# Residual stream with tokens on partitions, and the last down and out contractions swept half by half over all five token tiles

## The chip, the cores and the metric

The kernel runs on one core of one Trainium2 chip. The time is device microseconds of one execution, from the first to the last instruction of the core. The kernel before took 2431.77 us, the median of 3 runs (2429.27 to 2432.41).

## The reference

One inference step of a diffusion trunk of two layers (DEPTH = 2) with a width of 1024 (D_MODEL), over 128 prompt tokens and 512 latent tokens. Shift, scale and gate of every norm come from the conditioning vector, one for the prompt and one for the latent tokens. The attention and retention mixers between `h` and `branches` are left out here; the change does not touch them.

```python
def rmsnorm(x, gain):
    y = xf * lax.rsqrt(jnp.mean(xf * xf, axis=-1, keepdims=True) + NORM_EPS)
    return y * gain
...
    h = rmsnorm(x, g_mix) * (1 + scale1) + shift1      # then x_in = h @ w_in, four mixers
    ...
    gates = jax.nn.sigmoid((h @ p['w_gate'] + p['b_gate']).reshape(b, l, N_BRANCH, D_MODEL))
    mixed = jnp.sum(gates * branches, axis=2) @ p['w_out']
    x = x + gate1 * mixed
    h2 = rmsnorm(x, p['g_ffn']) * (1 + scale2) + shift2
    u = h2 @ p['w_up'] + p['b_up']                     # then a width-3 convolution over tokens
    a, gg = jnp.split(conv, 2, axis=-1)
    x = x + gate2 * ((jax.nn.silu(gg) * a) @ p['w_down'])
...
    y_prompt = rmsnorm(xp, g_final); y_sample = rmsnorm(xs, g_final)
```

## The kernel before, in words

There are 640 tokens in T = 5 tiles of 128: tile 0 is the prompt, tiles 1 to 4 the latent tokens. A width of 1024 is KD = 8 blocks of 128 channels. Every large product is made from three fp32r matmuls: the activation and the weight are each split into a high part (a rounded copy, `h_hi`, `a_hi`, `w_hi`) and a low part (the remainder, `h_lo`, `a_lo`, `w_lo`), and high by high, low by high and high by low are summed in PSUM. A weight unit is loaded into one of three `raw` buffers by the SP queue (1 MB), rounded into `w_hi` by ACT (line 1436) and subtracted into `w_lo` by POOL (line 767, four instructions); only the first two units of a layer's in-product are subtracted by DVE (line 1899). The order of every engine is written out by hand, with semaphores between the engines; SP loads the units in one fixed order (`weight_units`).

The residual `x` stands with channels on partitions, `[128, 8, 640]`. The norm over channels is therefore a sum over partitions: DVE squares and adds up the eight blocks (`add_square`, lines 2222 and 2224), PE sums over partitions with a vector of ones (`token_sums`, `part_sums`), ACT takes the root, DVE the reciprocal on a diagonal (line 1874), and PE spreads it over the partitions (`spread_rstd`, `spread_part`). DVE then makes scale times x times that (line 1883), ACT adds the shift and rounds into `h_hi` (line 1471), DVE makes `h_lo` (line 1891), block by block, and the first product (`in_product(0)`, line 914, groups of 512 columns per token tile) follows block by block. Layer 1's vectors (biases, gains, taps) are turned on PE at the boundary (`turn_vectors`, line 780), and the modulation of the norm (`mod_pair`, line 841, and `fold_pair`, line 850) is made around the start of each layer's first product.

Products on the residual's side have the weights as the stationary operand and the tokens as the moving one. The out product makes block m as two matmuls of 320 tokens for each of eight k; its last three blocks are split by tokens into 256 and 384, so that the first up tiles (`first_up`) can start on tokens 0 to 255 while the rest is added. The up and down products of the MLP run in three groups of up tiles, 8, 8 and 6 (`UP_GROUPS`), the down product of a group (`down_part`, columns of 322 and 320) two up tiles behind (`AHEAD`). DVE adds gate times the product to x (`add_to_x`, line 2230). At the start x is loaded with tokens on partitions and turned (40 transposes, line 791), and at the end it is turned back (40 transposes, line 1404) for the final norm (line 2333) and the stores.

## Time and profile before

| | us |
|---|---|
| median of 3 runs | 2431.77 |
| lowest, highest | 2429.27, 2432.41 |
| the profiled execution | 2432.2 |
| its span in the profile | 2430.4 |
| PE busy | 2363.8 |
| DVE, ACT, POOL busy | 1244.4, 879.1, 731.8 |
| mean granted clock of TensorE | 0.993 |

The profile page gives busy times and a chain of waits: the work that ended last, followed back to what released it at each step. The waits view tells how long PE stood idle and which engine's instruction released it. The timeline and the windows show one stretch. All times in them are from the start of the span, which is 1.8 us shorter than the execution's own time.

### The profile page before, as it was taken

To read this page: it belongs to the slowest core of one execution; us is meant where nothing else is said; L and a number is where in the kernel's file an instruction comes from. 1 tells how busy PE (TensorE), PEld (TensorE's weight loads), DVE (VectorE), ACT (ScalarE), POOL (GpSimd) and SP (SyncE) were. 2 spreads that over 40 slices of the span, in tenths; PEclk is the share of its full clock that TensorE was granted. 3 is DMA by queue.
4 is the path that set the end of the run, shared out by engine and by line. 5 is a ranking of instruction groups with operands and counts; after the bars stand their busy time and mean duration, and the time that the engine had idled before them with its cause. 6 is when DMAs were issued, how large, how long until landed. Compare 5 with 4: busy or idle time off the path is not lost.

```text
span 2430.4 us, 38405 instructions
## 1 busy us (share of the span) xinstructions
PE 2363.8 (97%) x16085; PEld 2144.0 (88%) x16085; DVE 1244.4 (51%) x2251; ACT 879.1 (36%) x1642; POOL 731.8 (30%) x500
## 2 busy tenths in 40 slices
PE   7999999999999999999999999999999999999998
PEld 5887787788999999999978878887889999999997
DVE  5426247534347762753763362673433677447356
ACT  4335245534324431332243352555343243223231
POOL 0321221101342453444312203210113435435432
PEclk9999999999999999999999999999999999999999
DMA  8413221222331322222271132312232312222211
GB/s 291 143 55 122 66 91 59 74 70 87 109 92 53 104 70 70 87 70 61 79 269 55 53 124 72 102 46 71 87 104 85 98 53 70 87 70 70 87 53 53
DMA packets 234154, 216.48 MB, mean 89 GB/s; under 512 B 8310, under 2 KB 217598, under 8 KB 233726
## 3 DMA queue, kind: packets, MB, share of 16 engines
q1 hardware_dynamic: 225911, 193.77, 25.0%
q10 hardware_dynamic: 8071, 20.25, 2.4%
q8 instruction: 128, 2.10, 0.3%
q14 instruction: 44, 0.36, 0.0%
HBM read 204.92 MB, written 9.08 MB: 88 GB/s over the span
## 4 chain that ended last, share of the span: by engine, by line
PE 88%; DVE 5%; ACT 3%; POOL 2%; issue 1%; DMA 0%; ACTq 0%; DVEq 0%
PE ps L819 58%; PE ps L914 11%; PE ps L968 4%; PE ps L1021 2%; POOL w_lo L767 2%; PE ps L1038 2%; PE ps L1000 2%; PE ps L1010 2%; PE ps L829 1%; ACT w_hi L1436 1%; DVE h_lo L1891 1%; PE ps L989 1%; DVE t L1883 1%; PE ps L859 1%; PE ps L1214 1%
## 5 line engine op out<-in xcount | busy, mean ns | idle before, releaser
L767 POOL TENSOR_TENSOR w_lo<-raw,w_hi 128x512 fp32r<-128x512 f32 x488 | 718.9, 1503 | 1664.3 <-ACT w_hi L1436 1048.8
L819 PE MATMUL ps<-h_hi,w_hi 128*128 128x320 f32 (+2 forms) x2368 | 618.4, 314 | 4.0 <-POOL w_lo L767 4.0
L819 PE MATMUL ps<-h_lo,w_hi 128*128 128x320 f32 (+2 forms) x2368 | 608.8, 310 | 0.0
L819 PE MATMUL ps<-h_hi,w_lo 128*128 128x320 f32 (+2 forms) x2368 | 608.7, 310 | 0.0
L819 PEld LDWEIGHTS ps<-h_hi,w_hi 128*128 128x128 f32 x2368 | 415.1, 189 | 8.8 <-issue 4.3
L819 PEld LDWEIGHTS ps<-h_lo,w_hi 128*128 128x128 f32 x2368 | 415.0, 189 | 0.8
L819 PEld LDWEIGHTS ps<-h_hi,w_lo 128*128 128x128 f32 x2368 | 415.0, 188 | 0.0
L1436 ACT ACTIVATE w_hi<-raw 128x2048 fp32r<-128x2048 f32 (+2 forms) x110 | 203.7, 1851 | 307.3 <-PE ps L819 219.0
L1986 DVE TENSOR_REDUCE stat<-ps 128x1 f32<-128x640 f32 (+3 forms) x160 | 107.9, 674 | 174.7 <-PE ps L1010 113.9
L914 PE MATMUL ps<-w_hi,h_hi 128*128 128x512 f32 (+1 forms) x480 | 182.8, 381 | 6.8 <-DVE h_lo L1891 3.8
L914 PE MATMUL ps<-w_hi,h_lo 128*128 128x512 f32 (+1 forms) x480 | 180.1, 375 | 0.0
L914 PE MATMUL ps<-w_lo,h_hi 128*128 128x512 f32 (+1 forms) x480 | 180.1, 375 | 0.0
L2230 DVE SCALAR_TENSOR_TENSOR x<-ps,mod,x 128x128 f32<-128x128 f32 (+4 forms) x192 | 72.9, 434 | 192.7 <-PE ps L819 192.0
L819 PE MATMUL ps<-a_hi,w_hi 128*128 128x322 f32 x704 | 162.6, 312 | 2.2 <-DVE a_lo L2297 1.4
L2282 DVE TENSOR_SCALAR conv<-u_pad,vcol 128x642 f32<-128x642 f32 x88 | 91.9, 1044 | 141.4 <-ACT u_pad L1788 139.8
L819 PE MATMUL ps<-a_hi,w_lo 128*128 128x322 f32 x704 | 161.7, 311 | 0.0
L819 PE MATMUL ps<-a_lo,w_hi 128*128 128x322 f32 x704 | 161.4, 310 | 0.0
L1796 ACT ACTIVATE usig<-conv 128x642 f32<-128x642 f32 x44 | 32.7, 744 | 261.3 <-DVE conv L2286 261.3
L968 PE MATMUL ps<-o_t,w_br 128*128 128x320 f32 x384 | 125.3, 450 | 0.0
L819 PEld LDWEIGHTS ps<-a_hi,w_hi 128*128 128x128 f32 x704 | 118.9, 190 | 3.3 <-DVE a_lo L2297 1.9
L2284 DVE SCALAR_TENSOR_TENSOR conv<-u_pad,vcol,conv 128x642 f32<-128x642 f32 x88 | 118.4, 1345 | 3.1
L819 PEld LDWEIGHTS ps<-a_lo,w_hi 128*128 128x128 f32 x704 | 118.8, 189 | 0.0
(299 smaller groups left out, 3330.0 us busy)
## 6 DMA issues: line engine op xcount, KB each, us to landing
raw<-in_w_mod SPq DMA_DIRECT2D x48, 1024.0 KB, 5.1
raw<-in_w_up SPq DMA_DIRECT2D x88, 512.0 KB, 4.6
raw<-in_w_gate SPq DMA_DIRECT2D x32, 1024.0 KB, 5.7
raw<-in_w_in SPq DMA_DIRECT2D x20, 1024.0 KB, 5.5
raw<-in_w_down SPq DMA_DIRECT2D x16, 1024.0 KB, 5.2
w_br<-in_w_branch ACTq DMA_DIRECT2D x8, 1024.0 KB, 5.0
raw<-in_w_out SPq DMA_DIRECT2D x8, 1024.0 KB, 5.2
raw<-in_w_down SPq DMA_DIRECT2D x8, 768.0 KB, 4.8
```

The costliest lines, as they stand in the source:

```text
L767: ins = nc.gpsimd.tensor_tensor(w_lo[part_slot(li, s)][:, c0:c1], raw[u % RAW][:, c0:c1], w_hi[part_slot(li, s)][:, c0:c1].bitcast(F32), A ...
L819: ins = mm(out, w_at(w_hl[wi]), at_(x_hl[xi]), start=first and q == 0, stop=final and q == 2)
L914: last = mm(bank(b, 0, n), (h_hi, h_lo)[xi][:, k, t * P:(t + 1) * P], w_hl[wi][:, k4, :], start=k == 0 and q == 0, stop=k == KD - 1 and q ...
L968: last = mm(bank(FILL_BANK[("branch", q)], 0, HALF), w_br[:, k, m * P:(m + 1) * P], o_t[n % 2][:, k, half * HALF:(half + 1) * HALF], start ...
L1000: last = mm(bank(2 * m2, col, col + n), query(br, t, h, m2), keys(br, h, m2, k0, n), start=True, stop=True)
L1010: last = mm(bank(2 * (m % 2), col, col + n), query(br, t, h, 0), keys(br, h, 0, k0, n), start=True, stop=True)
L1021: last = mm(ps[64 * odd:64 * odd + 64, 6 * BANK + 64 * h:6 * BANK + 64 * h + P], values(br, b, h + odd), turned(a_ + odd)[:, j, :], start= ...
L1436: act_(w_hi[part_slot(li, s)][:, 0:n], raw[u % RAW][:, 0:n], ACT.Copy).then_inc(hi_done.sem, 1)
L1986: V.tensor_reduce(stat[:, 0, col], bank(b, 0, nk), AX.X, ALU.max).then_inc(vstep.sem, 1)
L2230: ins = stt(x[:, k, c0:c0 + n], src, mod[:, gate0 + k, w:w + 1], x[:, k, c0:c0 + n], ALU.mult, ALU.add)
L2282: ts(cv, u[:, 0:PADDED], col(WCONV[0]), col(BCONV), ALU.mult, ALU.add).then_inc(vstep.sem, 1)
L2284: stt(cv, u[:, 1:1 + PADDED], col(WCONV[1]), cv, ALU.mult, ALU.add).then_inc(vstep.sem, 1)
```

## The change

The residual becomes `[128, 5, 1024]`, tokens on partitions; `acc`, the mixers' sum, gets a name of its own in the same memory. In the out and down products the activations (128 tokens of `mix_hi` or `a_hi`) are now stationary and 512 columns of the weights moving, so a weight unit is a half of the output columns (`dh`) by a half of the contraction (`kh`). The last output half of both, `dh = 1`, is made in two sweeps, each over all five tiles (`SWEEPS`). The norm is made per tile of tokens: ACT squares with a running sum and takes the root, DVE the reciprocal, ACT scales, PE turns eight blocks into PSUM (`turn_rows`), DVE modulates from PSUM, ACT rounds, DVE subtracts. Sums, diagonals and spreads go, as do the transposes at the start and at the end. The gates along channels are written to DRAM as rows and loaded back broadcast over partitions (`gate_rows`, `grow`). The four mod pairs of layer 1 are made among the down products of layer 0 (`PAIR_AT`), with their loads at the same place of SP's order. `ACT_SLOTS` goes from 12 to 10. The core of the diff:

```diff
-ACT_SLOTS = 12
+ACT_SLOTS = 10
...
+PAIR_AT = {(0, 0, 0): 0, (0, 0, 1): 1, (1, 0, 0): 2, (1, 0, 1): 3}
...
+ROW_BANK = ((0, 1, 2, 3, 4), (0, 1, 5, 6, 7))
+TURN_BANK = {"in": ((2, 3), (1, 4), (3, 5), (6, 7), (4, 5)), "ffn": ((2, 3), (0, 1), (4, 5), (2, 3), (6, 7))}
+SWEEPS = ((0, (0, 1, 2, 3, 4)), (1, (0, 1, 2, 3, 4)))
...
+                def turn_rows(layer, which, t):
+                    pe.wait_ge(xn_done.sem, ROW_BASE[layer, which] + t + 1)
+                    if t >= 2:
+                        pe.wait_ge(t1_done.sem, TURN_BASE[layer, which] + t - 1)
+                    if which == "in" and t == 3:
+                        pe.wait_ge(x_down.sem, counts(layer - 1)(x_down, n_down))
+                    if which == "ffn" and t == 4:
+                        pe.wait_ge(x_out.sem, counts(layer)(x_out, 2 * T))
+                    for k in range(KD):
+                        last = tr(bank(TURN_BANK[which][t][k // 4], k % 4 * P, k % 4 * P + P), xn[:, t % 2, k * P:(k + 1) * P], ident)
+                    last.then_inc(turn_mm.sem, 1)
...
+                if li == 0:
+                    turn_channels(0)
+                    mod_pair(0, 0)
+                    turn_channels(1)
...
+                else:
+                    first_product({(0, 0): lambda: turn_rows(li, "in", 3), (0, 1): lambda: turn_rows(li, "in", 4)})
+                    turn_vectors(7)
+                    pe.wait_ge(vec_done.sem, now(vec_done, 1))
                 in_product(1)
...
+                def out_sweep(dh, kh, tiles):
...
+                            for q, (xi, wi) in enumerate(((0, 0), (0, 1), (1, 0))):
+                                last = mm(bank(b), (mix_hi, mix_lo)[xi][:, k, row_cols(t)], w_hl[wi][:, k4, :],
+                                          start=k == 0 and q == 0, stop=k == KD - 1 and q == 2)
...
+                        if dh == 1 and (kh, t) in ((1, 2), (1, 3), (1, 4)):
+                            turn_rows(li, "ffn", {(1, 2): 0, (1, 3): 1, (1, 4): 2}[kh, t])
...
+                out_sweep(0, 0, range(T))
+                out_sweep(0, 1, range(T))
+                for kh, tiles in SWEEPS:
+                    out_sweep(1, kh, tiles)
...
+                        if (j, tokens, k) == (0, 0, 3):
+                            turn_rows(li, "ffn", 3)
+                        if (j, tokens, k) == (1, 0, 0):
+                            turn_rows(li, "ffn", 4)
...
+                        at_ = slice(t * P + (t > 0), t * P + (t > 0) + P)
+                        for k4 in range(nk):
+                            k = kh * nk + k4
+                            if dh == 0 and t == 0:
+                                pe.wait_ge(al_done.sem, now(al_done, j0 + k + 1))
+                            sl = (j0 + k) % ACT_SLOTS
+                            for q, (xi, wi) in enumerate(((0, 0), (0, 1), (1, 0))):
+                                last = mm(bank(b), (a_hi, a_lo)[xi][:, sl, at_], w_hl[wi][:, k4, :],
+                                          start=k == 0 and q == 0, stop=k == nj - 1 and q == 2)
...
+                    down_sweep(g, dh, kh, range(T))
+                    if (g, dh, kh) in PAIR_AT and li + 1 < DEPTH:
+                        pe.wait_ge(up_done.sem, now(up_done, min(FFT, sum(UP_GROUPS[g]) + AHEAD)))
+                        if (g, dh, kh) == (0, 0, 0):
+                            turn_mod_vectors()
+                        mod_pair(li + 1, PAIR_AT[g, dh, kh])
...
+                def norm_rows(layer, which, add, between):
+
+                    rstd = lambda t: row_rstd(ROW_BASE[layer, which] + t + 1, t)
+                    add(0)
+                    add(1)
+                    rstd(0)
+                    rstd(1)
+                    add(2)
+                    rstd(2)
+                    row_modulated(layer, which, 0)
+                    row_modulated(layer, which, 1)
+                    between()
+                    row_low(layer, which, 0)
+                    row_low(layer, which, 1)
+                    add(3)
+                    row_modulated(layer, which, 2)
+                    rstd(3)
+                    row_low(layer, which, 2)
+                    add(4)
+                    rstd(4)
...
+                def add_rows(t, dh, parts, gated, done, n):
+
+                    cols = slice(dh * BANK, dh * BANK + BANK)
+                    tt(parts[:, n % 2, :], bank(ROW_BANK[dh][t]), grow[:, min(t, 1), cols], ALU.mult).then_inc(gated.sem, 1)
+                    ve.wait_ge(gated.sem, now(gated, n))
+                    tt(x[:, t, cols], x[:, t, cols], parts[:, n % 2, :], ALU.add).then_inc(done.sem, 1)
```

PE at the boundary of the two layers, before: the last down matmul, the vectors' transposes (line 780), a mod pair (841), the sums (866), the fold (850), the spread (873), another pair and the first in-product (914).

```order
L819 MATMUL ps<-a_hi,w_lo_57 128x320
L780 MATMUL ps<-const,rows 128x96 [waits rows_loaded,x_after_mlp]
...
L841 MATMUL ps<-raw_52,cond_c 32x256 [waits raw_loaded0]
...
L866 MATMUL ps<-ones,ss 128x1 [waits squares_ready0,x_after_mlp]
...
L850 MATMUL ps<-const,mod_row 128x4 [waits mod_row_ready]
...
L873 MATMUL ps<-diag,ones 128x128 [waits rstd_diagonal,mod_ready]
...
L914 MATMUL ps<-w_hi_56,h_hi 128x512 [waits w_low_by_vector,h_ready,x_ready,vectors_ready]
```

PE at the same place, now: the turns of rows (line 889) stand behind the last down tiles (line 1386) and behind the first in tiles (905), the vectors' transposes (801) behind the whole first product, and the second in-product (938) behind them.

```order
L1386 MATMUL ps<-w_hi_56,a_lo 128x512
L889 MATMUL ps<-const,xn 128x128 [waits row_normed]
...
L889 MATMUL ps<-const,xn 128x128 [waits modulated,row_normed]
...
L905 MATMUL ps<-w_hi_57,h_hi 128x512 [waits h_ready,w_low_by_vector,w_low_ready]
...
L889 MATMUL ps<-const,xn 128x128 [waits x_after_mlp,modulated,row_normed]
...
L801 MATMUL ps<-const,rows 128x96
...
L938 MATMUL ps<-w_hi_57,h_hi 128x512 [waits w_low_ready,vectors_ready]
```

The mod pairs, sums and spread are gone from there; the vectors have moved from ahead of the first product to behind it.

DVE at the same boundary, now: residual adds (lines 2293 and 2295), reciprocals (1885), modulation from PSUM (1941), the weights' low half (1980), `h_lo` (1947).

```order
L1941 TENSOR_SCALAR hn<-ps,scl,mod 128x128 [waits normed_turned]
L1941 TENSOR_SCALAR hn<-ps,scl,mod 128x128 x7
L1980 TENSOR_TENSOR w_lo_59<-raw_54,w_hi_57 128x1024 [waits w_high_ready]
L1947 TENSOR_TENSOR h_lo<-hn,h_hi 128x8x128 [waits h_high] x2
L2293 TENSOR_TENSOR part_down<-ps,grow 128x512 [waits down_product]
L2295 TENSOR_TENSOR x<-x,part_down 128x512 [waits down_gated]
...
L1873 COPY vcol<-ps 128x317 [waits vectors_transposed,vector_step]
...
L2110 COPY decay<-decay 64x4 [waits small_loaded,vector_step]
```

The adds of tiles 3 and 4 stand behind the low parts of tiles 0 and 1; before, all adds stood ahead of the first modulation.

ACT in the norm of the MLP, now: the weight round (line 1455) stands between the scaled rows (1497) and the first rounded copies (1502).

```order
L1490 ACTIVATE xn,st_82<-x 128x1024 [waits x_after_mixers]
L1492 ACT_TABLE_LOAD
L1492 ACTIVATE st_82<-st_82,eps_c 128x1 [waits row_squares]
...
L1497 ACTIVATE xn<-x,st_82 128x1024 [waits row_rstd] x2
...
L1455 ACTIVATE w_hi_56<-raw_55 128x2048 [waits out_first_half,raw_loaded2]
L1502 ACTIVATE h_hi<-hn 128x8x128 [waits modulated] x2
```

Before, ACT read and rounded block by block (line 1471) behind one root for all tiles.

## Rows read from the trace of the kernel before

**Rows 1.** The page, its span, part 1 and part 4 (shares of the chain).

```profile
span 2430.4 us, 38405 instructions
...
PE 2363.8 (97%) x16085; PEld 2144.0 (88%) x16085; DVE 1244.4 (51%) x2251; ACT 879.1 (36%) x1642; POOL 731.8 (30%) x500
...
PE 88%; DVE 5%; ACT 3%; POOL 2%; issue 1%; DMA 0%; ACTq 0%; DVEq 0%
```

**Rows 2.** Waits of PE, whole span: total us, times, longest us.

```profile
PE ps L819 <- POOL w_lo L767: 4.9, 6, 1.3
...
PE ps L914 <- DVE h_lo L1891: 3.8, 2, 3.6
```

**Rows 3.** Chain of waits, pieces: start us, us, what, times in row.

```profile
679.90 5.14 PE ps L819 x35
...
790.85 381.98 PE ps L819 x2592
...
1186.89 2.05 PE ps L819 x12
...
1195.59 21.67 PE ps L819 x144
...
1227.86 1.62 PE ps L914 x6
...
1253.13 0.08 DVE decay L2041
...
1256.22 5.03 POOL w_lo L767 x4
1261.30 27.49 PE ps L914 x120
```

**Rows 4.** Chain of waits at the start, columns as in Rows 3.

```profile
13.59 6.39 PE ps L791 x40
...
28.30 6.16 PE ps L914 x15
34.45 1.86 PE ps L841 x32
...
61.23 5.04 POOL w_lo L767 x4
```

**Rows 5.** Timelines, DVE at 740 and PE at 775: start us, us, engine, line.

```profile
740.08 2.04 DVE L1891 SCALAR_TENSOR_TENSOR h_lo<-t,mod,h_hi 128x128 fp32r<-128x128 f32 x2
742.15 0.60 DVE L1883 SCALAR_TENSOR_TENSOR t<-x,scl,ps 128x128 f32<-128x128 f32 x2
742.67 0.61 DVE L1891 SCALAR_TENSOR_TENSOR h_lo<-t,mod,h_hi 128x128 fp32r<-128x128 f32 x2
...
775.87 0.45 PE L819 MATMUL ps<-h_hi,w_hi 128*128 128x320 f32 x2
```

**Rows 6.** Groups by form: ACT in 12:29, then DVE whole: busy us, mean ns.

```profile
L1417 ACT ACTIVATE y_tm<-x_tm 128x1024 f32<-128x1024 f32 x5 | 5.2, 1046 | 5.9 <-DMA x_tm<-in_x_sample 5.9
...
L1482 ACT ACT_TABLE_LOAD x1 | 1.3, 1283 | 0.0
...
L2224 DVE TENSOR_TENSOR ss<-ss,sq 128x640 f32<-128x640 f32 x22 | 28.4, 1291 | 0.8
...
L2138 DVE TENSOR_TENSOR st_dec<-ps,dmask 128x512 f32<-128x512 f32 x10 | 6.9, 692 | 30.6 <-PE ps L1101 30.6
```

**Rows 7.** Windows: us, busy PE, PEld, DVE, ACT, POOL, granted clock, DMA, GB/s.

```profile
28.00:34.00 6.00, 5.70 (x14) 4.53 (x15) 2.74 (x4) 0.00 (x0) 0.00 (x0) 0.53 0.53 177
...
1217.00:1262.00 45.00, 41.52 (x293) 31.17 (x292) 31.78 (x79) 19.38 (x33) 5.02 (x4) 1.00 0.87 314
```

**Rows 8.** Page, part 3: packets, MB, share of 16 engines.

```profile
q1 hardware_dynamic: 225911, 193.77, 25.0%
```

**Rows 9.** Timeline of the tail, columns as in Rows 5.

```profile
2411.78 0.31 PE L819 MATMUL ps<-a_hi,w_lo 128*128 128x320 f32 x1
...
2422.02 5.08 DVE L2333 SCALAR_TENSOR_TENSOR y_tm<-ps,st,g_fin 128x1024 f32<-128x1024 f32 x4 [0.35 <-PE ps L1404]
```

815 lines of the change are left out of this document (388 added, 427 removed).

## The prediction

> **What bounds the kernel now.** I read the page first, then PE's waits, then the chain of waits at the places that the change touches. PE is busy 97% of the span and the chain is PE for 88% [rows 1]; its largest waits on other engines' work inside the layers come to 4.9 and 3.8 us in total [rows 2]. So the time is PE's work in order plus the few places where PE has no work that is ready, and the change is to be judged by both. The profiled execution took 2432.2 us (span 2430.4); the sum is made against it, and the median 2431.8 lies 0.4 below. I count from marks: start of the second in-product (66.3 = 61.23 + 5.04, when POOL's w_lo is ready) [rows 4]; start of the out product (685.0 = 679.90 + 5.14) and start of the third up tile (775.9) [rows 3, 5]; start of layer 1's second in-product (1261.3) [rows 3]; last down matmul (2412.1) and end (2430.4) [rows 9, 1].
>
> **PE's rates.** A 512-column matmul takes 27.49/120 = 0.229 us; an up or down matmul of 320 or 322 columns 381.98/2592 = 0.147 in the long piece and 21.67/144 = 0.150 in the last downs, where all are downs [rows 3]; a transpose 6.39/40 = 0.16 [rows 4].
>
> **Down and up.** Before, a layer has 1056 down matmuls: at 0.149, between the two rates, 157.3 us. After, 660 of 512 columns: 151.1, so -6.2 a layer. The third group starts with the last up tile's activation missing: that tile ends at 1172.8 and its product starts at 1186.9 [rows 3], 14.0 us, of which PE fills all but 0.7 with other down work. After, one tile's wait for a_lo is in the first sweep: only its five other k steps and nothing of m 0 to 2 lie ahead; I take the cover that is left as 11.7 (five 0.23 us triples, and two up tiles' tail) and so a wait of 2.3: +1.6. One POOL wait of 0.4 there goes. The mod pairs of layer 1 move into layer 0's downs: 4 x 2.0 = +8.0 (an old pair is 1.86 [rows 4]; a new one has twice the matmuls at a quarter of the columns; bounds 0.9 to 3.7). Their loads stand ahead of two down weight loads in SP's queue: a load lands some 5 us after its issue; between 0 and 5 I take 1.4 each, as the slot comes free one tile earlier: +2.8. Together 2 x (-6.2 + 1.6 - 0.4) + 8.0 + 2.8 = **+0.8**.
>
> **Out to first ups.** Before 775.9 - 685.0 = 90.8. After: 192 matmuls of 512 columns until tile 0 of the last sweep is done, 44.0. From there I wrote a timetable of the orders shown above. Prices: residual multiply and add 0.7 each (512 from PSUM 0.69; the 640 in SBUF has a mean of 1.29, mixed of 0.83 alone and about 1.8 beside POOL) [rows 6]; Square with its read 1.2 and the table load 1.28 once, which stands on the path behind the first Square [rows 6]; Sqrt 0.27, reciprocal 0.17, scaling 1.05, the copy to h_hi 1.05, h_lo 1.24; eight transposes 1.28; the eight modulations of a tile 2.1. For these eight the trace has no tensor_scalar from PSUM: the scalar_tensor_tensor from PSUM is 0.30 for each 128 columns [rows 5], so 2.4 at most, and 1.6 at 0.2 each as the low end; I take 0.26. The Trainium skill (VectorE: DVE Perf Modes, Why PSUM operands drop a tier) says that an fp32 operand in PSUM keeps DVE at 1x, where one in SBUF could go at 2x; by it the high end would hold, 1.2 us more in each of three stages. No run here shows it yet.
> The timetable, from the end of tile 0: x is summed at 1.7, its square at 2.9, root at 4.5 (table load between), xn at 7.1. PE is through with tiles 1 and 2 at 5.5, so it waits 1.7 for the first turn. Tile 4 is done at 15.3, turn 2 at 16.6. DVE modulates tiles 0 and 1 until 14.9, then h_hi of both (ACT, 16.0, behind the weight round) and h_lo until 19.5, with POOL in its way; so first_up waits 3.0. DVE is behind from then on: tile 3 of x is added only at 20.9, tile 4 at 28.1. PE waits 2.0 before turn 3, 1.8 before turn 4, and 1.6 for h_lo of tile 4 (38.9). End of the four first ups: 55.9, of it 10.1 of waits. 44.0 + 55.9 - 90.8 = +9.1; the POOL wait before the fourth up tile (0.7 of 4.9 [rows 2]) goes, as PE comes to that tile later than its weights. (The wait of 1.0 for gprod at the start of the out product goes too; it is in the 90.8.) **+8.4 a layer, +16.8.**
>
> **Layer boundary.** Before, from the end of the last down matmul (1195.59 + 21.67 = 1217.3) to 1261.3: 44.0 [rows 3]. After, the same timetable with tiles of nine matmuls (2.06 us, so less cover): a wait of 3.1 before the first turn, 3.0 before the first in tile (its weights' low half is DVE's too), and 8.0 before turn 3, which needs the banks of down tiles 3 and 4 and therefore DVE's last residual add, done only at 28.8. The first product ends at 56.2; with the tiles after tile 0 taken off (4 x 2.06 = 8.2), 48.0 behind the last down matmul. Then the vectors: PE turns all 317 columns now, DVE copies them, and only behind that DVE starts the decay chain that ACT waits for before it rounds the next weights; 1253.13 to 1261.30 is 8.2 us [rows 3], which before lay beside PE's work and is now beside nothing. With 1.6 for turning and copying: 9.8. 48.0 + 9.8 - 44.0 = +13.8. The clock: at the start PE waits 3.6 us for h_lo [rows 2] and then runs at a granted 0.53 [rows 7], so at 1.2 GHz for a time: 15 matmuls took 6.16 instead of 3.44 [rows 4], 2.7 us. In the boundary before, with PE busy 41.5 of 45 us, it stayed at 1.00 [rows 7]. I count one such fall, behind the 9 us wait, +2.7. **+16.5.** By the Trainium skill (TensorE: Matmul & The Clock Gate, HAM oscillation) every longer idle gap between bursts brings the clock back to its low level; the 8.0 wait would then cost as much again, and the first start [rows 7] agrees with it.
>
> **Start.** The sums by token fall away, but channels are turned in the middle of the product. The last scaled row is there at about 23.3 (squares end 19.7, five roots, table load), the first turn, the pair, modulation, high and low give a first matmul at 30.5 against 28.30 [rows 4]. The product itself: 120 x 0.229 with its slow beginning 30.4, three pairs 6.0, six turns of five 4.8 (bank 5 alone, each waits for the one before), 2.2 of wait for channel 6; end 73.9. The vector and weight chain of 8.2 starts with the last h_lo and ends at 75.8, against 66.3: **+9.5.**
>
> **Tail.** Before 2430.4 - 2412.1 = 18.3, with sums, table load, 40 transposes and four products of 1.27 [rows 9]. After, no PE work: DVE has 1.4 + 0.2 + 1.28 for each of five tiles, begins at the end of tile 0 (-8.2) and ends 7.9 behind the last matmul; the last store needs the 3.3 that it needs now. 11.2: **-7.1.**
>
> **Sum.** 0.8 + 16.8 + 16.5 + 9.5 - 7.1 = +36.5: 2468.7, at the median 2468.
>
> **Rivals.** (a) *The row work hides* (faster): if ACT and DVE finish each row before PE needs it, the waits of 10.1 twice, 14.1 + 9.8 + 2.7, 4.1 at the start and 2.8 go, 53.7 in all; 2415. It decides at h_lo of tiles 0 and 1 before 16.6, when PE is through with its turns; mine is at 19.5, and the other tiles stand behind it in DVE's order. Half of the waits gone would be 2441.
> (b) *The clock falls at more waits*: also at 8.0, at 3.1 and 3.0, and in both ffn norms: 2 to 6 times 2.7 more, 2474 to 2484.
> (c) *Cheaper rows*: modulation 1.6, POOL not in DVE's way (4 less in three stages), the mod pair at 0.9 to 1.5, no queue wait: 2446 to 2460. Against the middle part stands [rows 5]: a low pair is 2.04 beside POOL's work and 0.61 without.
> (d) *The gate rows block SP's queue*: 4,096 elements of 4 bytes per layer ahead of the w_out loads. 0.25 x 16 engines x 2430 us over 225,911 packets [rows 8] is 43 ns each, 11 us over 16 engines; the load has some 23 us of slack in my reading of its issue. If they went over a few engines only, 44 us or more: w_out late by 20 in each layer, 2508.
> (e) *Nothing moves*: the wider matmuls and the tail pay for what is left of the waits. That needs two thirds of the 53.7 to be gone: 2432.
>
> **Chances.** Forecast (2460 to 2473) 0.45; (b) 0.18; (c) 0.20; (d) 0.05; (a) 0.09; (e) 0.03. The range leaves out (a) and (e) and most of (d): 2442 to 2486. A measurement of this kernel can tell about 0.2% (4.9 us) from no change: faster 0.09, same 0.03, slower 0.88.
>
> **What would show it.** Right: PE waits for h_lo, xn and x (down add) at every norm, some 10 us in each ffn norm and some 24 at the boundary; the granted clock below 1.00 at the boundary; DVE's eight modulations near 2.1; a tail of 11; out plus down matmuls at 0.229. Wrong: turn 3 waits for nothing (DVE's order was cheaper), or no wait before the second in-product, or 512-column downs slower than 0.229, which read their weights from odd columns of a_hi.

## The result, and the profile after

The changed kernel takes 2496.81 us, the median of 4 runs (2493.3 to 2501.8), against 2430.52 for the kernel before beside it (4 runs): the ratio is 1.0274, with an interval of 1.0254 to 1.0294. The change costs 66 us. The profiled execution has a span of 2495.4 us, 65.0 above the 2430.4 of [rows 1].

The page's span, part 1 and part 4, as in [rows 1]:

```profile
span 2495.4 us, 37639 instructions
...
PE 2360.1 (95%) x15742; PEld 2066.5 (83%) x15742; DVE 1234.7 (49%) x2169; ACT 901.8 (36%) x1644; POOL 735.3 (29%) x506
...
PE 85%; DVE 6%; ACT 4%; DMA 3%; POOL 1%; issue 1%; SPq 0%; DVEq 0%; ACTq 0%
```

PE is busy for 3.7 us less than before and the span is 65 us longer: all of the loss is time in which PE is idle, 68.7 us more of it. The waits that the view lists add up to 124.2 us, against 60.7; the other 5 us are gaps that it does not list. The waits view of PE, whole span (total us, times, longest us), its largest rows:

```profile
PE ps L831 <- DVE w_lo L2276: 17.2, 2, 10.4
PE ps L831 <- DVE h_lo L1947: 12.1, 4, 3.5
PE ps L938 <- POOL w_lo L788: 11.0, 2, 9.1
PE ps L876 <- DVE xn L1891: 9.7, 1, 9.7
...
PE ps L889 <- DVE x L2295: 6.4, 1, 6.4
...
PE ps L1386 <- POOL w_lo L788: 4.8, 2, 2.7
PE ps L1386 <- DVE a_lo L2334: 4.4, 2, 2.2
```

The row for h_lo at the first up tiles is 12.1 us now; the same view of the kernel before has for it (its line 819):

```profile
PE ps L819 <- DVE h_lo L1891: 1.7, 4, 0.7
```

The h_lo row of 3.8 in [rows 2] is another one, that of the in-products. The rows for h_lo, xn and x are the norm by rows, L938 on POOL is the wait for the vectors, the two rows of line 1386 are the downs: the forecast named all of these waits. It had nothing for the first row: 17.2 us in two waits for the low half of the last branch's weights (line 2276).

The second thing that it had too small is PE's clock. Over windows of 10 us I summed PE's busy time times one less the granted clock, the share of the time that was given up at a lower clock: 24.9 us, against 13.5 before. So PE's work at full clock would have got about 15 us shorter (-3.7 in busy time, and 11.4 of lower clock hidden in it), and its listed waits got 63.5 us longer.

The chain of waits, pieces at the marks of [rows 3, 4] (start us, us, what):

```profile
77.64 27.51 PE ps L938 x120
...
646.04 58.62 PE ps L831 x384
704.66 44.81 PE ps L1314 x192
...
788.74 129.68 PE ps L831 x864
...
1316.41 29.00 PE ps L938 x120
...
1946.51 44.81 PE ps L1314 x192
```

The second in-product of layer 0 starts at 77.6 (before 66.3), the out product at 704.7 (685.0), the second part of the first ups (line 831, x864) at 788.7, layer 1's second in-product at 1316.4 (1261.3), its out product at 1946.5 (1879.9). From these and the starts of the third up tiles (805.6 and 2047.5, before 775.9 and 1970.7) the loss by stretch:

| stretch | before | after | difference | forecast |
|---|---|---|---|---|
| start to second in-product | 66.3 | 77.6 | +11.3 | +9.5 |
| to out product, layer 0 | 618.7 | 627.0 | +8.3 | 0 |
| to third up tile | 90.8 | 101.0 | +10.1 | +9.1 |
| to last down matmul (turns and waits inside the last sweep taken off) | 441.4 | 452.3 | +10.9 | +5.1 |
| to layer 1's second in-product | 44.0 | 58.5 | +14.5 | +16.5 |
| to out product, layer 1 | 618.6 | 630.1 | +11.5 | 0 |
| to third up tile | 90.8 | 101.0 | +10.1 | +9.1 |
| to last down matmul (the same) | 441.4 | 437.3 | -4.1 | -5.7 |
| to the end | 18.3 | 10.6 | -7.7 | -7.1 |
| all | 2430.4 | 2495.4 | +65.0 | +36.5 |

The two stretches that the forecast had at nothing make 19.8 of the 28.5 us that it missed. (By place, 2.7 of the 16.5 forecast for the boundary, the slow clock behind the vectors' wait, belong to the stretch after it: so the boundary had 13.8 and took 14.5, and the second of the two stretches had 2.7 and took 11.5.)

**The branch weights.** The timeline at 618 to 650 (start us, us, engine, line, operation):

```profile
618.72 6.02 SPq L757 DMA_DIRECT2D gate_rows<-mod  x4
...
621.65 0.40 ACTq L1571 DMA_DIRECT2D w_br<-in_w_branch  x1
...
641.66 1.91 ACT L1795 ACTIVATE w_hi<-w_br 128x2048 fp32r<-128x2048 f32 x1 [12.18 <-DMA w_br<-in_w_branch]
...
643.61 2.29 DVE L2276 TENSOR_TENSOR w_lo<-w_br,w_hi 128x2048 fp32r<-128x2048 f32 x1 [16.95 <-ACT w_hi L1795]
...
646.04 0.87 PE L831 MATMUL ps<-o_hi,w_hi 128*128 128x320 f32 x2 [10.35 <-DVE w_lo L2276]
```

SP issues the four writes of the gate rows at 618.7, ACT the load of the last branch's weights at 621.7. The load has landed at 641.7; ACT rounds it, DVE subtracts, and PE has waited 10.35 us at 646.0. The DMA view of 600:660 (KB each, median us to landing), and below it the same view of the kernel before at 590:650:

```profile
w_br<-in_w_branch ACTq DMA_DIRECT2D x1, 1024.0 KB, 20.0
...
gate_rows<-mod SPq DMA_DIRECT2D x4, 4.0 KB, 15.9
```
```profile
w_br<-in_w_branch ACTq DMA_DIRECT2D x1, 1024.0 KB, 4.8
```

The writes move 4 KB each and take 15.9 us; the load beside them takes 20.0 instead of 4.8. It came 15.2 later and PE waited 10.4, so this load had about 4.9 us of slack. In layer 1 the load took 16.5 us and PE waited 6.9. The 15.9 is the median of the four writes, each of 1,024 elements; the landings of all four (least, median, longest, from each one's issue):

```profile
DMA to landing us min/median/max: 12.1/15.9/21.4
```

The last of them, issued at 624.4, landed at 643.5, 24.8 us after the first was issued. The wait also costs clock: the 384 matmuls behind it took 58.62 us (59.11 in layer 1), where at the rate of the same product in e1 below (70.54 us for 480) they take 56.4.

**The norm by rows.** The chain at the layer boundary:

```profile
1252.57 1.28 ACT L1492
...
1259.48 5.09 DVE hn L1941 x16
...
1266.14 2.27 DVE h_lo L1947 x2
...
1276.38 1.81 DVE x L2295
...
1278.33 1.94 PE ps L889 x8
...
1311.33 4.95 POOL w_lo L788 x4
```

In order: ACT's table load behind the first Square, two tiles' modulations on DVE (5.09 us for 16), their h_lo, the last residual add (1.81 us while POOL makes a low half from 1276.37 on, 0.69 two tiles before with POOL idle), and only then PE's turn 3 at 1278.33. At the end POOL makes the low half of the second in-product's weights, done at 1316.3; PE, through with the vectors' turn, has waited 9.1 for it. Groups of DVE by form (busy us, mean ns):

```profile
L2295 DVE TENSOR_TENSOR x<-x,part_down 128x512 f32<-128x512 f32 x60 | 57.6, 959 | 2.0
...
L1941 DVE TENSOR_SCALAR hn<-ps,scl,mod 128x128 f32<-128x128 f32 x120 | 39.2, 400 | 0.4 <-PE ps L889 0.4
...
L1947 DVE TENSOR_TENSOR h_lo<-hn,h_hi 128x1024 fp32r<-128x1024 f32 x15 | 21.1, 1423 | 13.2 <-ACT h_hi L1502 13.2
```

The windows view (us, busy PE, PEld, DVE, ACT, POOL, granted clock, DMA share, GB/s) shows where the clock goes:

```profile
640.00:660.00 20.00, 13.96 (x81) 13.99 (x82) 7.54 (x7) 6.66 (x6) 4.97 (x4) 0.74 0.42 127
1260.00:1280.00 20.00, 9.81 (x45) 7.73 (x43) 16.11 (x33) 11.34 (x14) 6.14 (x5) 0.80 0.16 52
1316.00:1326.00 10.00, 9.59 (x36) 7.84 (x37) 7.40 (x11) 4.09 (x15) 5.22 (x5) 0.81 0.68 210
```

Each of these windows holds one of the waits above or follows it, and has a mean granted clock of 0.74 to 0.81, so part of it was run at 1.2 GHz; the boundary before stood at 1.00 [rows 7].

### The profile page after: what moved, and what is told of

The parts are those of the page before. It is cut to its first block, busy times and chain, and to the rows that moved or that the text cites. A ratio compares the mean times of both kernels' runs of the same rounds, so it can differ in the third digit from the quotient of the medians.

```text
span 2495.4 us, 37639 instructions
## 1 busy us (share of the span) xinstructions
PE 2360.1 (95%) x15742; PEld 2066.5 (83%) x15742; DVE 1234.7 (49%) x2169; ACT 901.8 (36%) x1644; POOL 735.3 (29%) x506
## 3 DMA queue, kind: packets, MB, share of 16 engines
q1 hardware_dynamic: 218871, 193.80, 24.9%
## 4 chain that ended last, share of the span: by engine, by line
PE 85%; DVE 6%; ACT 4%; DMA 3%; POOL 1%; issue 1%; SPq 0%; DVEq 0%; ACTq 0%
PE ps L831 42%; PE ps L938 10%; PE ps L1386 10%; PE ps L992 4%; PE ps L1314 4%; PE ps L1045 2%; PE ps L1062 2%; PE ps L1024 2%; PE ps L1034 2%; DMA w_br<-in_w_branch 1%; POOL w_lo L788 1%; DVE hn L1941 1%; PE ps L842 1%; PE ps L905 1%; DMA raw<-in_w_down 1%
## 5 line engine op out<-in xcount | busy, mean ns | idle before, releaser
L1386 PE MATMUL ps<-w_hi,a_hi 128*128 128x512 f32 x440 | 174.8, 397 | 9.2 <-POOL w_lo L788 4.8
L938 PE MATMUL ps<-w_hi,h_hi 128*128 128x512 f32 (+1 forms) x440 | 166.7, 379 | 17.4 <-POOL w_lo L788 11.0
L1386 PE MATMUL ps<-w_lo,a_hi 128*128 128x512 f32 x440 | 174.2, 396 | 0.0
L1386 PE MATMUL ps<-w_hi,a_lo 128*128 128x512 f32 x440 | 174.1, 396 | 0.0
L2319 DVE TENSOR_SCALAR conv<-u_pad,vcol 128x642 f32<-128x642 f32 x88 | 90.1, 1024 | 156.3 <-ACT u_pad L1830 154.7
L938 PE MATMUL ps<-w_lo,h_hi 128*128 128x512 f32 (+1 forms) x440 | 164.2, 373 | 0.0
L938 PE MATMUL ps<-w_hi,h_lo 128*128 128x512 f32 (+1 forms) x440 | 164.2, 373 | 0.0
L1830 ACT ACTIVATE u_pad<-ps,vcol 128x128 f32<-128x128 f32 (+3 forms) x264 | 91.6, 447 | 91.7 <-PE ps L831 91.7
L2323 DVE SCALAR_TENSOR_TENSOR conv<-u_pad,vcol,conv 128x642 f32<-128x642 f32 x88 | 116.7, 1326 | 3.1
L2321 DVE SCALAR_TENSOR_TENSOR conv<-u_pad,vcol,conv 128x642 f32<-128x642 f32 x88 | 116.6, 1325 | 3.1
L1600 ACT ACTIVATE probs<-ps,stat 128x640 f32<-128x640 f32 (+3 forms) x136 | 90.2, 664 | 67.7 <-DVE stat L2063 67.1
```

What stands on the lines that cost most here:

```text
L938: last = mm(bank(b, 0, n), (h_hi, h_lo)[xi][:, k, t * P:(t + 1) * P], w_hl[wi][:, k4, :], start=k == 0 and q == 0, stop=k == KD - 1 and q ...
L1386: last = mm(bank(b), (a_hi, a_lo)[xi][:, sl, at_], w_hl[wi][:, k4, :], start=k == 0 and q == 0, stop=k == nj - 1 and q == 2)
L1600: act_(prob(m)[:, 0:nk], bank(score_bank(m), 0, nk), ACT.Exp, bias=bias, scale=SCALES[br], accum_out=stat[:, 2, m % 8:m % 8 + 1]).then_inc ...
L1830: ins = act_(u[:, d0:d0 + n], bank(b, c0, c0 + n), ACT.Identity, bias=bias)
L2321: stt(cv, u[:, 1:1 + PADDED], col(WCONV[1]), cv, ALU.mult, ALU.add).then_inc(vstep.sem, 1)
L2323: ins = stt(cv, u[:, 2:2 + PADDED], col(WCONV[2]), cv, ALU.mult, ALU.add)
```

## The experiments

All times are medians of 4 runs beside runs of the kernel before on the same chip. e1 to e4 shared a chip, and so did e5 to e8, e9 to e12, and e13 with e14; between these groups compare the ratios. An interval reaches 0.0015 to 0.0024 to either side, 4 to 6 us, so many of the smaller steps are read from the stretches of the trace. The last two columns are of the profiled execution, in us: what PE gave up at a lower clock, as above, and the sum of PE's waits. That execution is not always near the median: e5's took 2475.1 us, the longest of its four, e8's 2464.3 and e14's 2455.1, the shortest of theirs.

| kernel | median us | ratio, 95% interval | at low clock | waits of PE |
|---|---|---|---|---|
| before | 2429.3 to 2430.5 | 1 | 13.5 | 60.7 |
| changed | 2496.8 | 1.0274, 1.0254 to 1.0294 | 24.9 | 124.2 |
| e1 rows behind w_br | 2482.5 | 1.0214, 1.0198 to 1.0229 | 20.9 | 109.2 |
| e2 rows twice | 2510.5 | 1.0330, 1.0311 to 1.0348 | 26.2 | 135.9 |
| e3 vectors early | 2492.7 | 1.0255, 1.0236 to 1.0273 | 28.7 | 115.3 |
| e4 sweeps split | 2498.2 | 1.0275, 1.0259 to 1.0290 | 28.9 | 124.5 |
| e5 = e1 + e3 | 2469.3 | 1.0164, 1.0147 to 1.0181 | 21.5 | 98.3 |
| e6 = e5 + turns later | 2474.7 | 1.0183, 1.0168 to 1.0198 | 25.7 | 97.0 |
| e7 = e6 + modulate first | 2471.8 | 1.0172, 1.0157 to 1.0188 | 21.1 | 98.3 |
| e8 = e5 + sweeps split | 2468.7 | 1.0160, 1.0143 to 1.0177 | 15.6 | 102.0 |
| e9 = e5 + idle filled | 2470.9 | 1.0172, 1.0155 to 1.0189 | 18.5 | 88.5 |
| e10 = e5 + table ahead | 2472.8 | 1.0172, 1.0157 to 1.0188 | 27.1 | 97.0 |
| e11 = e5 + second pair in sweep | 2468.6 | 1.0158, 1.0142 to 1.0173 | 23.1 | 97.5 |
| e12 = e8 + e10, e11, shorter e9 | 2461.8 | 1.0136, 1.0113 to 1.0160 | 14.1 | 90.2 |
| e13 = e5 + first pair in sweep | 2466.1 | 1.0149, 1.0134 to 1.0165 | 24.2 | 95.2 |
| e14 = e8 + e10, e13, e7's order on DVE | 2461.4 | 1.0133, 1.0116 to 1.0150 | 14.7 | 94.3 |

### The gate rows behind the branch weights (e1, e2)

```diff
                         sp.wait_ge(mod_done.sem, now(mod_done, 20))
+                        sp.wait_ge(branch_loaded.sem, now(branch_loaded, 16 * NB))
                         for v in range(2):
```

> One edit to the changed kernel: SP waits until the last branch weights (w_br) have landed before it issues the four writes of the gate rows. Theory A (the 4-byte writes share the rings with the w_br load and made it land after 20.0 us instead of 4.8): PE's waits of 10.4 and 6.9 us for DVE's w_lo go, the load lands in about 5 us, and the time falls by 15 to 18 us to about 2480. The first w_out load then comes later (writes 16 us, load 5) but has some 50 us until it is needed, so no new wait. Rival B (the w_br load is late because ACT issues it later in the changed kernel, or because of the weight loads beside it): the load still takes about 20 us and the time stays at 2497. Rival C (w_out becomes late instead): the waits go, but PE waits some 10 us before the out product, net change under 8 us.

Measured 2482.5, -14.3. The DMA view of e1 at 600:660:

```profile
w_br<-in_w_branch ACTq DMA_DIRECT2D x1, 1024.0 KB, 5.0
```

and the chain of waits, the same product as at 646.04 above:

```profile
626.00 70.54 PE ps L832 x480
```

The load lands in 5.0 us, and the wait of PE is gone in both layers. The stretches from the second in-product to the out product take 617.3 and 619.9 us, against 627.0 and 630.1 with the change and 618.7 and 618.6 before: the whole of the unforeseen loss in these stretches was due to the writes beside this load, and 19.9 us come back. Of them some 5 do not show in the median. In the profile the start is 1.6 us longer, the downs of layer 0 0.6 and the last downs 1.5; for the last the granted clock is lower (0.90 and 0.93 in 2430:2450, where the changed kernel has 1.00), for the start it is not, and that stays open. Theory A holds, with 14.3 us for the 15 to 18 expected. Rivals B and C fall: PE does not wait ahead of the out product. With no load beside them the elements of layer 0 are moved within 12 us: the DMA view of e1 at 631:643 counts 4,155 packets under 512 B. That is the price that the forecast had for them, 11 us.

e2 issues each write a second time, into a DRAM tensor that nothing reads:

```diff
+                                sp.dma_start(gate_again[li, v, c_].rearrange("(k p) -> p k", p=P), mod[:, 16 + 24 * v:24 + 24 * v, c_],
+                                             allow_slow_non_contiguous=True).then_inc(again.sem, 16)
```

> One edit to the changed kernel: each of the four gate-row writes per layer is issued twice, the second time to another DRAM tensor that nobody reads. Theory A (these writes hold the rings, about 16 us for 4,096 elements): 4,096 more elements hold them some 16 us longer, the w_br load lands after about 36 us, and PE waits some 16 us longer in each layer: 2496.8 + 2 x 16 = about 2529. Rival B (the cause of the late load is another one): within 4 us of 2497. If the load overtakes the second half of the writes, the rise is less than half of theory A's.

```profile
PE ps L835 <- DVE w_lo L2280: 27.1, 2, 15.4
```
```profile
w_br<-in_w_branch ACTq DMA_DIRECT2D x1, 1024.0 KB, 21.3
...
gate_rows<-mod SPq DMA_DIRECT2D x4, 4.0 KB, 28.1
```

and of layer 1, at 1840:1900 (16.5 with the change):

```profile
w_br<-in_w_branch ACTq DMA_DIRECT2D x1, 1024.0 KB, 25.1
```

The timeline in layer 0:

```profile
622.04 0.40 ACTq L1575 DMA_DIRECT2D w_br<-in_w_branch  x1
...
625.22 18.00 SPq L758 DMA_DIRECT2D gate_rows<-mod  x1
...
643.39 1.91 ACT L1799 ACTIVATE w_hi<-w_br 128x2048 fp32r<-128x2048 f32 x1 [13.51 <-DMA w_br<-in_w_branch]
```

The waits grow from 17.2 to 27.1 us and the time by 13.7. The direction is theory A's, the size is not: it is less than half of the 32, the case that the expectation names for a load that overtakes the second half of the writes. SP gets four of the eight transfers out by 625 and then stands in the issue of the next for 18.00 us, until 643.2, when the load has landed too (21.3 after its issue). My reading, which no run tests by itself: the load is held up only by the writes that were issued by then, four as in the changed kernel, and the rest falls on what comes later: the w_out loads take 21.3 us here. That fits layer 0, where the load takes 1.3 us more and PE's wait grows from 10.4 to 11.7. It does not explain layer 1: there SP stands in its fifth issue for 19.6 us just so, and yet the load takes 8.6 us more and the wait grows from 6.9 to 15.4. What sets the size stays open. Twice the elements cost 10 us more of PE's wait, not 32.

### Layer 1's vectors (e3, e5)

```diff
+                    def early_vectors():
+                        pe.wait_ge(t1_done.sem, TURN_BASE[li, "in"] + 4)
+                        turn_vectors(7)
-                    first_product({(0, 0): lambda: turn_rows(li, "in", 3), (0, 1): lambda: turn_rows(li, "in", 4)})
-                    turn_vectors(7)
+                    first_product({(0, 0): lambda: turn_rows(li, "in", 3), (0, 1): lambda: turn_rows(li, "in", 4), (0, 4): early_vectors})
```

> One edit to the changed kernel: PE turns layer 1's vectors behind the first half of the first product (after tile 4 of it, and when DVE has read row tile 3 from the same bank) instead of behind the whole product. Forecast's theory (DVE's copy and the decay chain, ACT's round and POOL's w_lo are 9.1 us that nothing covers, and the clock falls behind this wait): the wait of 9.1 before the second in-product goes, the slow clock behind it too (29.0 us for 120 matmuls back to 27.5), so -9 to -11 us, about 2486. Rival (another release sets that round: the raw load, the slot of the first in weights, or DVE's h_lo of tile 4, done late): the wait shrinks by less than 4 us, 2493 to 2497.

Measured 2492.7, only 4.1 less, and with runs from 2487.4 to 2498.2. In the trace the wait of 9.1 for POOL is gone, and 120 matmuls of the second in-product take 27.20 us instead of 29.00:

```profile
1165.52 56.33 PE ps L831 x384
...
1315.50 27.20 PE ps L938 x120
```

From 1165.52 (the last up tiles) to there it is 150.0 us, against 158.8 with the change: -8.8 in place, close to the -9 to -11 expected. From there to layer 1's out product it is 3.6 less, half of it the faster matmuls. What the median does not show was given back where the kernels do not differ: +4.7 between the first layer's second in-product and its out product, +2.8 in its ups and downs. Why, these two traces do not say for certain; the time given up at a lower clock is 3.8 higher in e3. e5 puts both edits together:

> The changed kernel with two edits together: gate rows written only when w_br has landed (-14.4 us alone) and layer 1's vectors turned behind the first half of the first product. Alone the second moved its own stretch (from the third group's up tiles to the second in-product) by 8.8 us in the trace, but the median by 4.1 only. Theory (the gains are of separate places and add; the missing part was scatter of the w_br wait and of the clock behind it, which the first edit takes out): 2482.5 - 9 = 2473.5, and runs that scatter by less than 4 us. Rival (the vectors' gain is given back elsewhere): 2478 to 2482.

2469.3: -27.5 from the changed kernel, -13.2 from e1, more than the two medians alone add up to (14.3 + 4.1) and near what the stretches add up to (19.9 + 8.8). In e5's own trace the boundary is 152.5 us, 6.3 less than with the change and not 8.8: the last downs ahead of the norm took 23.33 us for 93 matmuls there, 21.88 with the change. The theory's number (2473.5) lies 4 above; that the runs scatter by less than 4 us was wrong (2466.8 to 2475.1).

### The split of the sweeps (e4, e8)

```diff
-SWEEPS = ((0, (0, 1, 2, 3, 4)), (1, (0, 1, 2, 3, 4)))
+SWEEPS = ((0, (0, 1, 2)), (1, (0, 1, 2)), (0, (3, 4)), (1, (3, 4)))
```

> One edit to the changed kernel: the last output half of out and down, and the first in-product of layer 1, run over tiles 0 to 2 (both halves of the contraction) and then over tiles 3 and 4, instead of each half over all five. Theory (sweeping each half over all five tiles leaves only two tiles' work between the end of tile 0 and the first turn, and DVE gets tiles 0 to 2 too late): tile 0 is done 6 x 2.75 us of matmuls, not 4 x 2.75, before the end in out, so 5.5 us (out) and 4.1 us (down) more cover in each of the two ffn norms, the boundary and the tail; the waits for xn at turn 1 or later and for h_lo of tiles 0 and 1 go (3.5 + 3.8 and parts of the rest), together -3 to -5 us per norm, -10 to -14 in all: about 2485. Rival (DVE's total work per norm is the limit, not when tile 0 is done; or the weights' slots are released later and rounds come late): within 4 us of 2497, or slower by some 5 us for late w_lo of the first up tiles.

2498.2, no change. In place: from the start of the out product to the second part of the first ups 82.4 us in both layers, where it was 84.1; the boundary 157.6 for 158.8; the tail's stretch 1.4 less. So the split is worth 1.7, 1.2, 1.7 and 1.4, together 6, half of what the theory had. The waits for h_lo go from 12.1 to 9.4, and the one for DVE's last add grows from 6.4 to 7.9: with more work of PE ahead, DVE's own list of work is what is late. The rival is right on the median and in its reason. On top of e5:

> The kernel of the two edits together (gate rows behind w_br, vectors earlier), with the last out and down halves and the first product run over tiles 0 to 2 and then 3 and 4, as in e4. Alone this edit left the median where it was, though its stretches were 1.7, 1.2, 1.7 and 1.4 us shorter in the trace. Theory (the gain is real and was hidden by scatter of the w_br wait and the clock): -5 to -6 us against the kernel of the two edits, about 2468. Rival (no gain, as measured alone): within 2 us of that kernel.

2468.7 against 2469.3: not to be told from nothing by the median; the two stretches from the out product to the first ups are again 1.7 shorter each.

### The order inside the norm (e6, e7, e10)

e6 turns row tiles 3 and 4 behind tiles 1 and 2 of the first product (`(0, 1)` and `(0, 2)` in the dictionary); e7 also calls `row_modulated(layer, which, 0)` ahead of `rstd(2)` on DVE; e10 puts `act_(st5[:, 3, 0:1], eps_c[:], ACT.Sqrt)` ahead of `rms(0)` on ACT.

> The kernel of the two edits together (gate rows behind w_br, vectors earlier), with the turns of row tiles 3 and 4 in layer 1's first product one tile later (behind tiles 1 and 2 instead of 0 and 1). Theory (the wait of 6.4 us before turn 3 is DVE's last residual add; PE could do tile 1 in it): PE fills 2.75 us of that wait, and row tiles 3 and 4 are still in time, -2 to -3 us against that kernel. Rival (tiles 3 and 4 then come late by as much, since DVE's chain behind turn 3 sets their h_lo): within 1 us of it.

> The kernel before this one (gate rows behind w_br, vectors earlier, turns one tile later), with one more edit in all three norms by rows: DVE modulates row tile 0 before it takes the reciprocal of tile 2, for which it waits some 2 us while tile 0's turn is done. Theory (DVE's order, not its work, makes h_lo of tiles 0 and 1 late): -1 to -2 us in each of three norms, -3 to -6 in all, with PE's waits for h_lo lower by that. Rival (ACT's chain for tile 2 gets late by the modulation of 2.6 us and turn 2 waits instead): 0 to +3 us.

> The kernel of e5 with one root of a constant put ahead of the first Square in each norm by rows, so that ACT loads its table of 1.28 us while it waits for x. Theory (the table load stands on the path from the end of tile 0 to the first turn): PE's wait before the first turn falls by 1.3 us in each of three norms (2.6 to 1.3 in the boundary), and h_lo of tiles 0 and 1 by up to as much: -2.5 to -4 us in all. Rival (turn 0 earlier gives nothing as the later waits for h_lo and x grow by the same): within 1 us of e5 (2469).

e6: 2474.7, +5.4 on e5, and 154.1 us from the last up tiles to the second in-product where e5 has 152.5. The wait for x falls from 5.4 to 3.8 and the one for h_lo rises from 2.7 to 5.0: filling the wait helps nothing, as the tiles behind it are late by more. The theory's sign was wrong; the rival gives the reason, but had the time within 1 us. (The wait for x before turn 3 is 5.4 us in e5 and 6.3 to 6.6 in e1, e11 and e13, which have the same code there.) e7: 2471.8; its ffn stretch is 83.8 for 84.1, the boundary 153.7 for 154.1: 0.3 to 0.4 each, not 1 to 2. e10: 2472.8, slower by the median than e5 within the intervals; the boundary is 150.8 (-1.7), while the waits for h_lo in the ffn norms stay at 6.0. The table load is on the path to the first turn and hardly on the path to the first product. All three theories had too much. What they leave is that DVE's work in sequence (0.69 + 0.69, 2.55, 1.23 a tile) sets the end: the three show that these other orders gain little, and no run has less work on DVE, so this is argued and not shown.

### The clock (e9)

```diff
+                            if t == 4:
+                                for _ in range(12):
+                                    mm(bank(2), mix_hi[:, 0, 0:P], mix_hi[:, 1, 0:512], start=True, stop=True)
```

and the same with 10 and 20 matmuls in the boundary.

> The kernel of e5 (gate rows behind w_br, vectors earlier) with matmuls that nobody reads put on PE into three of its waits: 12 behind turn 2 of each ffn norm (2.7 us into the waits of 3.4 and 2.6 for h_lo), 10 at the same place of the boundary and 20 ahead of the wait of 5.4 us for turn 3. They are shorter than the waits, so they delay nothing that is on the path; what changes is that PE is not idle. Theory (part of the lost time is the granted clock, which falls behind these waits: 21.5 us of PE time given up at low clock in e5's trace against 13.5 in the kernel before): the granted clock in the boundary and behind the ffn norms stays nearer to 1.00 and the time falls by 3 to 6 us, 2463 to 2466. Rival (the clock does not depend on such short waits, or the falls come at other places): within 1.5 us of e5, or +1 to +3 where a filler overshoots its wait.

2470.9 against 2469.3. The time given up at the low clock goes from 21.5 to 18.5 us, and the boundary (152.7 for 152.5) and the ffn stretches (84.1 for 84.1) take what they took: PE's waits fall to 88.5, as the filling counts as work, and nothing comes of it. In the boundary the granted clock did rise, in windows of 10 us from 0.83, 0.67 and 0.81 (e5, from 1258) to 1.00, 0.83 and 1.00 (e9, from 1252), and the time did not fall: there the end is not set by PE's clock, and the theory falls. In the ffn norms the clock stayed where it was (0.83 in 761:771 of e5, 0.84 in 757:767 of e9), so that half was not tested. What the falls elsewhere cost, this run does not say.

### The mod pairs in layer 0's downs (e11, e13)

e11 makes the second pair of a group, e13 the first one, from within `down_sweep`, behind tile 3 and tile 2. The edit of e13, which stands ahead of the sweep's line for tile 3:

```diff
+                        if not kh and dh == 0 and t == 2 and (g, 0, 0) in PAIR_AT and li + 1 < DEPTH:
+                            pe.wait_ge(up_done.sem, now(up_done, min(FFT, sum(UP_GROUPS[g]) + AHEAD)))
+                            if g == 0:
+                                turn_mod_vectors()
+                            mod_pair(li + 1, PAIR_AT[g, 0, 0])
```

> The kernel of e5 with the second mod pair of each of the first two down groups of layer 0 put behind tile 3 of its sweep instead of behind tile 4, so that PE frees the raw buffer 2.75 us earlier in which the next down unit is loaded. Theory (the waits of 2.7 and 2.1 us for POOL's w_lo in layer 0's downs come from that buffer, held by the mod units until PE reads them): both waits go or shrink below 0.5, -4 us: about 2465. Rival (the load waits for SP's order or the mod loads' own arrival, not for PE's read): the waits stay and the time is within 1 us of e5.

The waits stay (4.2 for 5.0), 2468.6: the theory falls.

> The kernel of e5 with the first mod pair of each of the first two down groups of layer 0 (and the turn of its vectors) put behind tile 2 of the first sweep instead of behind tile 4. Theory (SP's queue waits for PE's read of the first pair's raw buffers before it issues the second pair's loads, and the third down unit's load stands behind those; the trace has that load 10.8 us from the first pair's read): the read comes 5.5 us earlier, so the two waits for POOL's w_lo (2.8 and 2.2 us) go below 0.5 each: -4 to -5 us, about 2465. Rival (as with the second pair, the waits stay at 4 to 5 us in all): within 1.5 us of e5, 2468 to 2471.

The chain of the changed kernel at 900:960, and below it that of e13:

```profile
918.42 13.88 PE ps L1386 x60
...
932.50 1.97 PE ps L855 x128
...
934.90 10.75 DMA raw<-in_w_down
...
945.67 1.93 ACT w_hi L1455
...
947.67 5.42 POOL w_lo L788 x4
...
953.13 6.92 PE ps L1386 x22
```
```profile
914.43 8.34 PE ps L1391 x36
...
922.97 1.92 PE ps L856 x128
924.89 19.74 PE ps L1391 x84
944.63 1.92 PE ps L856 x128
946.55 13.63 PE ps L1391 x58
```

With the change PE's read of the first pair (932.5) lets SP issue the second pair's loads and behind them the down weights, which land 10.75 us later; round and low half end at 953.1. In e13 the chain is PE from one end to the other, and both waits are gone. The ratio is 1.0149 where e5 has 1.0164, inside the intervals of the two; the trace settles it: from the second part of the first ups to the last up tiles of layer 0 it is 364.0 us for 370.6, of which 1.6 is one piece of matmuls that ran at a low clock in e5. The pairs themselves, 4 x 1.97 us, stay.

### All together (e12, e14)

> Gate rows behind w_br, vectors earlier, sweeps split 3 and 2, root table ahead (in the tail too), second pairs inside the sweep, and shorter fillers (4 behind turn 2 in each ffn norm, 3 in the boundary, 20 ahead of turn 3). Theory (the gains add): e8's 2468.7 less 3 (table), 4 (pairs), 3 (clock): about 2459, so still some 28 us slower than the kernel before, since the row norms' waits of about 8 us each, the start and the four moved pairs stay. Rival (more gains than that, each wait removed also keeps the clock up): 2450 or below; it would have to be below 2425 to beat the kernel before, which I do not expect.

> Gate rows behind w_br, vectors earlier, sweeps split 3 and 2, modulation of tile 0 ahead of tile 2's reciprocal, root table ahead (tail too), first pairs inside the sweep, no fillers. Theory (the parts add, and the fillers of e12 gave nothing): e8's 2468.7 less 3 (modulation), 2 (table), 4 (pairs): about 2460, like e12's 2461.8. Rival (without fillers the clock falls more often and takes it back): 2465 to 2469. Neither beats the kernel before.

2461.8 and 2461.4, 2.8 and 1.4 above what was expected (e12 holds the edits of e1, e3, e4, e9 with fewer matmuls, e10 with the same load ahead of the tail, and e11; e14 those of e1, e3, e4, e7's order on DVE, e10 and the tail, and e13). e14 comes out as fast as e12 without any filling. With e14 the changed kernel has 35 us of its 66 back and is 1.33% slower than the kernel before. The traces have less of it: the profiled execution of e14 is its fastest, with a span of 2453.3 us, 22.9 above the kernel before. In it PE waits 94.3 us instead of 60.7, 33.6 more, and is busy 13.2 us less. The largest of them that belong to the change are those of the rows' chain (10.3 for xn, 9.4 for h_lo, 6.3 for x), 9.3 for the first scaled rows and 5.3 ahead of the second in-products. No version ran that beats the kernel before.

## Why the prediction was wrong, point by point

The sign was right and the size was not: +36.5 forecast, +65 and +66 measured, 11 us beyond the range's end.

- **The gate rows' writes** are the step that failed. Rival (d) had them, asked only what they do to SP's own queue, and priced them at 43 ns an element, 11 us, with 23 us of slack in front of the w_out loads; the forecast itself put them at nothing. The price alone was fair (12 us in e1), and PE did not wait for w_out. But they hold up more than the queue of their issuer: ACT's load of the last branch's weights, issued 3 us behind the first of them, landed after 20.0 us (16.5 in layer 1) instead of 4.8, and the writes themselves took 24.8 from the first issue to the last landing. The chain of that load (round, subtract) had 4.9 us of slack. Asking which loads of other queues are in flight at that time, and which of those is needed next, was left out. Cost: 19.8 us in the stretches (e1). Without them the kernel takes 2482.5, inside the range. By what means the writes slow the load, no run shows.
- **Layer 0's downs**: +10.9, forecast +5.1. The waits for the down weights were 2.7 and 2.1 us, where 2.8 in all was forecast, by the mechanism named (SP's order), to which e13 adds that SP stands there until PE has read the first pair. A moved pair is 1.97, as taken. The 512-column matmul took 55.69/240 = 0.232 here, not 0.229: 2 us a layer. The rest, some 2 us, is at a low clock: 29.69 us for 120 matmuls at 953.13, where the next such piece has 28.11.
- **The last a_lo**: a wait of 2.2 us in each layer, forecast 2.3. Layer 1's downs, -4.1 for -5.7, differ by about the same: 0.232 makes 2.0. The prediction gave slower downs as a sign that reading weights from odd columns costs time; the out product, which does not read from there, has 44.81/192 = 0.233 too, so that is not the reason.
- **Out to first ups**: 56.1 us from the end of tile 0 to the third up tile, forecast 55.9; first turn after 6.8, forecast 7.2; waits for h_lo of 3.5 and 2.5 forecast as 3.0 and 1.6, 9.0 of waits in all for 10.1. The eight modulations are 2.55, for 2.1 taken, and above the high end of 2.4. There the Trainium skill (VectorE: DVE Perf Modes, Why PSUM operands drop a tier) was the better guide: no fast mode for fp32 in PSUM, and the 2.55 agree with it. But the 1.2 us a stage that the prediction put on this side of the choice did not come: the timetable behind tile 0 is 0.2 over. Of the +1.0 a layer, 0.8 is the out product, 44.81 us for the 44.0 forecast. That one total came out so near with single terms off by up to 1 us to either side is in part luck.
- **Boundary**: from tile 0's end (1249.9) to the second in-product 66.5 us, forecast 66.0 and 2.7 for the clock behind it, where 120 matmuls took 29.00 us for 27.49, 1.5. The wait for x was 6.4 (8.0), for the vectors 9.1 (9.8).
- **Start and tail**: +11.3 for +9.5, with the three pairs 1.9 each and a wait of 9.7 for the first scaled rows; -7.7 for -7.1.
- **The clock**: one fall of 2.7 forecast, 11.4 us more measured. The rule of the Trainium skill (TensorE: Matmul & The Clock Gate, HAM oscillation), that longer idle gaps between bursts bring the low level back, fits the windows above better than my count of one. The two waits for the branch weights brought 2.2 and 2.7 us of it (58.62 and 59.11 for 56.4), and e1, where they are gone, gives up 4.0 us less. But e9 shows that in the boundary the low clock is not the cause of the time. How much of the rest is on the path stays open; between runs of one kernel the granted clock and the time move together (e12: a run of 2458.8 at a mean granted clock of 0.992, one of 2471.9 at 0.989).

Rival (a) has no support: no wait of the row path was hidden. (b) is in part what happened. (c) was wrong in its main price, the modulation.

## What to carry to other kernels

A transfer of single 4-byte elements is not small: four of 4 KB took 12.1 to 21.4 us to land, and it delays the loads of other queues, so look for what is in flight beside it and needed next, not only for what stands behind it in its own queue. A norm that is moved from sums over partitions to rows removes small matmuls from PE but puts a chain of ACT and DVE behind the first finished tile, 18.5 us here until h_lo of the first two tiles is done (749.5 to 768.1, and 1249.9 to 1268.4); the PE work between that tile and the next product must be that long, and reordering it gave 1 to 2 us a norm, not more. Before a vector or constant is computed behind a product, look who waits for it two engines on: 9 us of cover were lost for a transpose of 0.4 us.

## What the hardware showed that I had not expected

- The load that ACT issued beside SP's element writes took 20.0 us for 1 MB (4.8 alone). With twice the writes it took 21.3 in layer 0 and 25.1 in layer 1 (16.5 with the change), and SP stood 18.0 and 19.6 us in one issue. So doubling them added 1.3 us in one layer and 8.6 in the other, and no run tells why.
- PE's granted clock fell in places where the kernels are the same: the 120 matmuls of layer 0's second in-product took 27.51 us in the changed kernel and 29.08 in e3, which differ only behind it. Differences under 5 us between two kernels here need their stretches, not their medians. Behind a long wait it is no scatter: the same 120 matmuls in layer 1 took 29.00, 30.23, 30.21 and 29.52 us in the four kernels in which PE waits 9.1 us just before them (changed, e1, e2, e4), and 27.20 in all eight in which that wait is gone (e3, e5, e6, e7, e9, e10, e11, e13).
- tensor_scalar from PSUM: 0.32 us for 128 columns, slower than the scalar_tensor_tensor of 0.30 that [rows 5] shows.
